# The first block's gate and up projections as two-level block products in quads, with the convolution by halves of tokens

## What is computed

```
D_FF = 2816
hn = rms_norm(h, norm_ffn_g)
gate = causal_depthwise_conv(hn @ w_ffn_gate, ffn_conv_w)      # 3 taps over tokens, per channel
h = h + (silu(gate) * (hn @ w_ffn_up)) @ w_ffn_down
```

## Time and profile before

| what | value |
|---|---|
| median of 3 runs | 3222.9 us (3221.6 to 3223.73) |
| span of the profiled execution, first to last instruction | 3218.1 us |
| median less that span | 4.8 us |
| PE, DVE, ACT, POOL busy over the span | 3120.3, 1809.7, 773.7, 1101.7 us |
| mean granted clock of PE | 0.989 of full speed |
| gate and up stage (L1936), first and last start | 806.1 and 1340.7 us |

### The profile page before, as it was taken

One profiled execution on the slowest core, in us unless ns is written; L12 is line 12 of the kernel. 1 busy time (PEld: TensorE's weight loads), 2 busy tenths in 40 slices (PEclk: granted clock), 3 DMA queues, 4 the chain that ended last, 5 costly groups with the idle time before them and its releaser, 6 DMA issues.

```text
span 3218.1 us, 32376 instructions
## 1 busy us (share of the span) xinstructions
PE 3120.3 (97%) x12306; PEld 1914.3 (59%) x12306; DVE 1809.7 (56%) x2558; ACT 773.7 (24%) x1302; POOL 1101.7 (34%) x855
## 2 busy tenths in 40 slices
PE   8997998999999999999999999999999999999997
PEld 3445564864444444588644554544554588888886
DVE  2386887742544434487634754753124655567877
ACT  3343334321111111000212333413212344410002
POOL 0010020003333333455610100152014698855655
PEclk9999999999999999999999999999999999999998
DMA  4220111241222122475312211102112233366652
GB/s 140 66 66 27 53 31 53 66 158 65 79 98 85 63 98 85 168 260 194 129 53 80 66 53 57 62 33 90 62 53 78 105 138 144 118 232 246 228 191 91
DMA packets 206121, 334.88 MB, mean 104 GB/s; under 512 B 10128, under 2 KB 123280, under 8 KB 205200
## 3 DMA queue, kind: packets, MB, share of 16 engines
q1 hardware_dynamic: 205968, 332.81, 29.8%
HBM read 268.55 MB, written 64.23 MB: 103 GB/s over the span
## 4 chain that ended last, share of the span: by engine, by line
PE 86%; DVE 8%; POOL 3%; ACT 2%; issue 1%; DMA 1%; DVEq 0%; POOLq 0%; SPq 0%; ACTq 0%
PE psum L1936 16%; PE psum L3767 15%; PE psum L181 10%; PE psum L3496 8%; PE psum L2555 8%; PE psum L407 7%; PE psum L1981 3%; PE psum L4334 3%; PE psum L563 1%; DVE arena L1380 1%; DVE arena L1378 1%; PE psum L3513 1%; PE psum L4311 1%; PE psum L4272 1%; PE psum L1987 1%
## 5 line engine op out<-in xcount | busy, mean ns | idle before, releaser
L3767 PE MATMUL psum<-arena 128*128 128x256 f32 x2660 | 579.4, 381 | 7.1 <-POOL arena L3793 7.1
L3767 PEld LDWEIGHTS psum<-arena 128*128 128x128 f32 x2660 | 506.7, 191 | 78.8 <-POOL arena L3793 8.6
L1936 PE MATMUL psum<-arena 128*128 128x512 f32 x1232 | 530.1, 592 | 1.9 <-DVE arena L2314 1.9
L1936 PEld LDWEIGHTS psum<-arena 128*128 128x128 f32 x1232 | 233.7, 190 | 296.6 <-issue 291.5
L407 PE MATMUL psum<-arena 128*128 128x512 f32 x768 | 337.9, 599 | 7.1 <-DVE arena L1236 4.9
L181 PE MATMUL psum<-arena 128*128 128x512 f32 x768 | 332.4, 592 | 1.5 <-ACT arena L4504 1.5
L2236 DVE TENSOR_TENSOR arena<-arena,psum 128x512 f32<-128x512 f32 x176 | 117.0, 686 | 296.3 <-PE psum L1936 154.7
L407 PEld LDWEIGHTS psum<-arena 128*128 128x128 f32 x768 | 146.2, 192 | 189.6 <-issue 185.0
L181 PEld LDWEIGHTS psum<-arena 128*128 128x128 f32 x768 | 145.8, 190 | 182.1 <-issue 180.6
L2555 PE MATMUL psum<-arena 128*128 128x512 f32 x576 | 251.7, 595 | 0.0
L3496 PE MATMUL psum<-arena 128*128 128x256 f32 x1080 | 244.6, 380 | 6.3 <-DVE arena L3541 5.6
(11 more groups left out here) (552 smaller groups left out, 4374.2 us busy)
## 6 DMA issues: line engine op xcount, KB each, us to landing
arena<-w_in SPq DMA_DIRECT2D x42, 1024.0 KB, 5.2
arena<-mlp_w SPq DMA_DIRECT2D x72, 512.0 KB, 7.0
arena<-w_ffn_down SPq DMA_DIRECT2D x36, 512.0 KB, 7.3
arena<-mlp_w SPq DMA_DIRECT2D x8, 2048.0 KB, 8.6
mlp_hidden_T<-arena SPq DMA_DIRECT2D x32, 512.0 KB, 2.6
arena<-mlp_hidden_T SPq DMA_DIRECT2D x16, 1024.0 KB, 5.6
arena<-w_out SPq DMA_DIRECT2D x12, 1024.0 KB, 5.2
mlp_hidden_B<-arena SPq DMA_DIRECT2D x24, 512.0 KB, 2.6
```

The costliest lines, as they stand in the source:

```text
L1936: mm = nc.tensor.matmul(ps, left, right, start=(k == 0), stop=(k == 3))
L3767: mm = self.env.nc.tensor.matmul(ps[:, 256 * r:256 * r + 256], left[:, s, r * P:(r + 1) * P], right[:, s, :], start=(first and s == 0 and ...
```

## The change

Gate and up become one product in the class `Quads`: a quad is 256 gate columns and the 256 up columns of the same pair, so eleven quads, quad 0 with plain items and ten with two levels. Items 1 and 2 of quad 1 run between those of quad 0. The loads are two of 1 MB per quad into one of two buffers. The seven items of a quad are added up on DVE (`combine`), seven sums of 128 x 1024.

The convolution is done per half of the tokens, for the two tiles of the pair: `conv(g, 0)` and `conv(g, 1)`. The second half needs the last two columns of the first, which are kept in `past`, and adds them with four small instructions. `silu` and `mul` are per half, too. The four sums of the hidden tile (T3, T1, T2, T4) move from POOL to DVE. The hidden tile and its sums have one buffer instead of three, so `conv(g, 0)` waits until pair g - 1 is stored. The order on DVE is written out by iteration n, where `added_after` says what follows an item: after an item of m1 = 1 both muls of the quad before, after 2 the four sums, after 6 U2 and C11, after 7 U3, after 5 U4 and C22, after 4 C21 and conv half 0, after 3 C12 and conv half 1. The first of these runs one iteration after its item, the others two.

The POOL queue now holds the level sums and outer sums of the quads. The rings reuse the table of constants, which is loaded again afterwards. The buffers of the down product move to other tiles, and what its loads and sums wait for changes: weights of items 0 and 1 are fetched when quad 9 is past. The first loads of "ple" wait for other events.

```
-            def conv(g, j):
-                i, from_, to = 2 * g + j, made["gate"][j], hid(j, g)
-                if g >= 3 and j == 0:
-                    dve.wait_ge(*stored(g - 3))
-                step.step(dve, v_.tensor_scalar(to, from_, tap(2, i), None, ALU.mult))
-                step.step(dve, v_.scalar_tensor_tensor(to[:, 1:T], from_[:, 0:T - 1], tap(1, i), to[:, 1:T], ALU.mult, ALU.add))
-                hidden.mark(v_.scalar_tensor_tensor(to[:, 2:T], from_[:, 0:T - 2], tap(0, i), to[:, 2:T], ALU.mult, ALU.add), "conv", g, j)
...
+            def conv(g, h):
+                if h == 0:
+                    if g:
+                        dve.wait_ge(*stored(g - 1))
...
+                hidden.wait(dve, ("C11", "C12")[h], g)
+                to, from_ = hid(h), (a_, c_)[h][g > 0]
+                taps = lambda j: [tap(j, 2 * g + r) for r in range(2)]
+                if h == 0:
+                    v_.tensor_copy(past, from_[:, :, HALF - 2:HALF])
+                for r in range(2):
+                    step.mark(v_.tensor_scalar(to[:, r, :], from_[:, r, :], taps(2)[r], None, ALU.mult))
+                base = step.n
+                for r in range(2):
+                    dve.wait_ge(tap_done, base - 1 + r)
+                    step.mark(v_.scalar_tensor_tensor(to[:, r, 1:], from_[:, r, 0:HALF - 1], taps(1)[r], to[:, r, 1:], ALU.mult, ALU.add))
+                for r in range(2):
+                    dve.wait_ge(tap_done, base + 1 + r)
+                    ins = v_.scalar_tensor_tensor(to[:, r, 2:], from_[:, r, 0:HALF - 2], taps(0)[r], to[:, r, 2:], ALU.mult, ALU.add)
+                if h:
+                    for r in range(2):
+                        step.mark(v_.scalar_tensor_tensor(to[:, r, 0:2], past[:, r, :], taps(0)[r], to[:, r, 0:2], ALU.mult, ALU.add))
+                    for r in range(2):
+                        dve.wait_ge(tap_done, base + 3 + r)
+                        ins = v_.scalar_tensor_tensor(to[:, r, 0:1], past[:, r, 1:2], taps(1)[r], to[:, r, 0:1], ALU.mult, ALU.add)
+                hidden.mark(ins, "conv", g, h)
...
+            added = [(name, q) for name in {6: ("U2", "C11"), 7: ("U3",), 5: ("U4", "C22"), 4: ("C21",), 3: ("C12",)}.get(m1, ())]
...
+            elif m1 in (3, 4):
+                added += {3: ends(q)[0:1] if q == 0 else ends(q)[1:2], 4: ends(q)[0:1] if q else []}[m1]
+            elif m1 in (1, 2):
+                added += {1: ends(q - 1)[2:4], 2: ends(q - 1)[4:]}[m1]
...
+            for n in range(LAST_N + 1):
+                if two_level(n - 1):
+                    quads.add_block(dve, n - 1, "c22")
...
+                for key in added_after(n - 2)[1:]:
+                    add_up(key)
+                if two_level(n):
+                    quads.add_block(dve, n, "c11")
+                    if n == LAST_N - 1:
+                        late.right_sums(dve, 0)
+                    quads.add_block(dve, n, "c12")
+                for key in added_after(n - 1)[:1]:
+                    add_up(key)
...
+            for q in PAIRS:
+                if q:
+                    store_pair(q - 1)
+                if q + 2 < 11:
+                    made_late.wait(sp, *quads.last_pass(at_item[q, 4]))
+                    p_sum.wait(sp, "S4", q)
+                    load_quad(q + 2)
+                elif q == 9:
+                    late.load_weights(sp, 0, before_late_load)
+                    late.load_weights(sp, 1, before_late_load)
```

More of the change, by code:

```diff
@@ L1832, in weights_of, with passed @@
             return down[:, q + 5 * c:q + 5 * c + n, j]
+        def passed(eng, m1):
+            made_late.wait(eng, *quads.last_pass(at_item[10, m1]))
         def before_late_bank(pe, at):
-            tiles.wait_free(pe, late_banks[at])
+            b = late_banks[at]
+            if at == 0:
+                tiles.wait_free(pe, b)
+                return
+            n, kind = max((n, m) for n in range(LAST_N - 3, LAST_N) for m in (1, 2, 3) if quads.bank_of(n, m) == b)
+            if kind == 1:
+                copy.wait(pe, "c21", n)
+            else:
+                hidden.wait(pe, {2: "c11", 3: "c12"}[kind], n)
@@ L2097, in _ @@
             hidden.wait(sp, "late", "S", 24)
-            load_unit(UNITS)
-            made_late.wait(sp, "late", 26, "all")
-            load_unit(UNITS + 1)
-            for v in range(UNITS + 2, len(sequence)):
-                after.wait(sp, *last_of(v - 2))
+            load_unit(0)
+            hidden.wait(sp, "late", "S", 25)
+            load_unit(1)
+            for v in range(2, len(ple_units)):
+                after.wait(sp, *ple_units[v - 2], 1)
                 load_unit(v)
@@ new lines, in combine @@
+            def combine(name, q):
+                a, b, c, d, e, f, b4 = [out_of(q, m1) for m1 in (1, 2, 6, 7, 5, 3, 4)]
+                before = {"C11": "U2", "U3": "C11", "U4": "U3", "C22": "U4", "C21": "C22", "C12": "C21"}
+                if name in before:
+                    hidden.wait(dve, before[name], q)
+                if name in ("U2", "U3", "U4", "C21", "C12"):
+                    quads.wait_product(dve, at_item[q, {"U2": 6, "U3": 7, "U4": 5, "C21": 4, "C12": 3}[name]])
+                to, one, two = {"U2": (c, a, c), "C11": (a, a, b), "U3": (d, c, d), "U4": (c, c, e), "C22": (e, d, e), "C21": (d, d, b4),
+                                "C12": (c, c, f)}[name]
+                hidden.mark(v_.tensor_tensor(to, one, two, ALU.add), name, q)
@@ L2420, in _, with more @@
-            for n in range(1, LATE):
+            def more(o):
+                made_late.wait(pool, *quads.last_pass(at_item[0, {"T3": 7, "T4": 4, "B22": 3}[o]]))
+                if o != "T4":
+                    hidden.wait(pool, "x", "T2", 1)
+                if o != "T3":
+                    hidden.wait(pool, "x", "T1", 1)
+                if o != "B22":
+                    pool.wait_ge(residual_out[0], residual_out[1] + 32)
+                quads.more_sums(g_, p_sum, pool, o)
+            add_sq(0, range(8))
```

575 lines of the change are left out of this document (306 added, 269 removed).

## The result

The changed kernel takes 3292.77 us (median of 4 runs, 3291.98 to 3293.28), the kernel before on the same chip 3222.25 (4 runs, 3220.01 to 3223.73): ratio 1.0219, 95% interval 1.0205 to 1.0234. The forecast was 3256 us and slower; the sign was right, the size was 37 us short, and the time lies 4.8 us above the range.

A forecast was written before the change was run, and what follows sets the result against it. PE was taken to bound the gate and up stage. 486.6 + 77 for DVE and its port + 5 for the tail = 568.6 against 535.0, +33.6, so 3256 us; range 3200 to 3288.

The forecast's parts named there:

- PE time removed: Gate and up stage: quad 0 at 48.1 us, ten quads at 42.6, norm about 2.1; PE work 476.1 us.
- bulge: PE's stall per quad from a late c22, as DVE and POOL take turns at SBUF; own range 6 to 10.5 us.
- the term "77 us": Gate and up stage: stalls of 8 us at nine places (quads 2 to 10) plus 5 for quad 0's convolution.
- start (quad 0's burst and quad 2's place): First quads of the stage: 5 us for quad 0's convolution among quad 1's items, 8 us for quad 2.
- the term 486.6: Gate and up stage without anything new: 476.1 us of PE work plus 10.5 of waiting, 48.4 less than before.
- my bound of 10.7: Stall at one place if nothing of POOL's passes under DVE's PSUM adds: 10.7 us; 0.5 if nothing is shared.
- the working: Stall at item (q, 2): DVE ends at 4.5 + 19.7 = 24.2 us, PE wants 15.5, so 8.7 us.
- The signs that I named: Stage over 535 us; 256-column matmuls near 0.217 apart except gaps of 3 and 5; taps 1.1 to 1.2; POOL stretched 15.
- The port costs little: Gate and up stage: PE held 1 us a quad or less; kernel at 3180 to 3190 us; chance 0.15.
- POOL becomes the pace: Gate and up stage: POOL's 44.8 us a quad sets the pace; stage 513.6, kernel 3202 us; chance 0.13.
- The tail goes worse: Down product: DRAM's round trip and the weights behind it cost 20 us more than forecast, 3276 us; chance 0.07.
- Loads, stores and ACT's copies at nothing: Gate and up stage: loads have 40 us to spare, copies are those of the second block; no cost.

The follow-up runs named there:

- e1: The changed kernel with the two earlier taps of the convolution left out, output not the reference's; 3182.18 us.
- e3: The changed kernel with dummy matmuls on PE ahead of its two long waits for c22, from the third quad on; 3285.25 us.
- spread kernel: The changed kernel with the convolution cut by rows over several DVE turns and C11 later, from the third quad on, same work; 3228.43 us.
- e5: The spread kernel with the last tap's scale on ACT for three of four rows a quad, all four in the first quad; 3222.83 us.
- e9: e5 with the first two quads spread by rows as well, the first convolution beginning one item earlier; 3216.49 us.
- e8: e5 with the sums T3 and C22 moved from DVE's fullest turns to emptier ones, from the fourth quad on; 3227.53 us.

## Why the prediction was right in sign and short in size

**PE time removed: right.** With its rivals for the port gone the stage is 493.7 us, against my 486.6 without bulge; the period is 42.56 against 42.6 a quad. PE was busy 481.5 us there, 5.4 above the 476.1 forecast, and waited 12.2 against 10.5. The 5.4 fit the clock, which the sum took as full: it is 0.74 from 886.9 to 900.0 and 0.87 from 916.4 to 930.0 in that kernel, behind waits of 5.5 and 2.7 us.

**The step that failed is the term "77 us" of the part on DVE and its port.** The stage holds 597.5 - 486.6 = 110.9 us in its place. By sections, against the kernel without taps:

| section | forecast | measured |
|---|---|---|
| base (stage of e1 less 486.6) | 0 | 7.1 |
| start (quad 0's burst and quad 2's place) | 5 + 8 | 15.8 |
| seven quads | 7 x 8 = 56 | 7 x 11.17 = 78.2 |
| last quad, to the down product | 8 | 9.8 |
| sum | 77 | 110.9 |

Without the base, which belongs to the term 486.6, the collision cost 103.8 us where 77 stood.

The mechanism is the one forecast: two engines by turns, c22 late at the items (q, 1) and (q, 2), PE released by L3656. The size per quad was 11.2, not 8, and even beyond my bound of 10.7. Of the 3.2 us missing per quad, 1.6 is the clock (period 53.7 against 52.1 with it kept up), a term that the sum did not have: I took every matmul at 0.2173. The other 1.6 is c22 itself: at full clock it costs 9.6 and not 8. 0.7 of that I gave away: the working came to 8.7 and I took 8 without a reason. The working itself was close. It has 19.7 us from S2 to the end of c22 of (q, 2), and at full clock it is 19.9 (e3); the pass behind it is 9.0 us late there. The last 0.6 come behind a c22 later in the quad, which I had not looked at. The waits as they stand in the profile (77.2 in the stage, 87.5 forecast with those of the start) look like a hit, but by chance: part of the bulge had become slow matmuls (520.75 us busy against 476.1), and these hid behind DVE.

**The signs that I named.** Gaps of "about 3 and 5": 3.04 and, in most quads, 3.3 to 3.9; right for the first. Taps at 1.1 to 1.2: 1.34. Adds from PSUM untouched: 0.417. POOL stretched by 15 us a quad: 266.5 us in seven quads are 38, 9 more than its 29.4. POOL waiting for PE: yes (2.69 before S2 above). The matmuls at 0.217 between gaps: wrong for 3.4 to 6.8 us behind most of the long gaps, where the clock is 0.50 (in the usual quad 3.4 behind the first and 6.8 behind the second).

**Rivals.** "The port costs little" fell with the result; its 3180 to 3190 is just where e1 came out, which is what the change would be worth without the collision. "POOL becomes the pace" fell with the waits: POOL is busy 266.5 of 382 us in the seven quads and waits for PE, and PE's waits there all name DVE's add; in e1, with all of POOL's sums, the period is 42.6. "The tail goes worse": the down product took 7.7 us more (forecast 5), not 20. 3.8 us more lie behind it: 2.4 in the second block's first MLP product (363.3 us against 360.9), 2.5 behind that, less 1.1 in between; their cause is open. Loads, stores and ACT's copies at nothing: right, but for 4.7 us in the start, where DVE waited for the first pair's store before it could write the next hidden half.

## What to carry to other kernels

When two engines take turns at a port, don't ask whether their busy times fit in the period; list what stands ahead of the instruction that the bound engine waits for, and spread that. Here the same instructions in other turns of the queue gave back 64 of 71 us. A wait behind which PE's clock falls costs more than its length, but not as much as the slow matmuls add up to when another engine is late meanwhile (here 1.6 us a quad came back, not 3): price it by keeping the clock up with dummies. Do not round a term of the sum down without a reason. And before moving an instruction to the emptiest turn of its engine, look at what the other user of the port has there.

## What the runs showed of the hardware

- A very small instruction of DVE with both tensors in SBUF can wait out a whole one of POOL. In the spread kernel an edge tap of one column took 2.27 us beside POOL's S3 of 2.36, against 0.22 alone. Timelines of DVE and POOL:

```profile
1074.89 2.27 DVE L2374 SCALAR_TENSOR_TENSOR arena<-small_sb,cols_sb,arena 128x1 f32<-128x1 f32 x1
```

```profile
1074.79 2.36 POOL L3723 TENSOR_TENSOR arena<-arena 128x1024 f32<-128x1024 f32 x1
```

- TENSOR_SCALAR with one tensor input takes its turns too: 1.03 us beside POOL, 0.479 without it.
- Whether the clock fell behind a wait did not go by the length of the wait alone. Two waits at the same place in two kernels, 2.13 us in e5 and 2.14 us in e9 (from the timelines), were followed by 0.62 in the first and by 1.00 in the second. Windows of e5, then of e9:

```profile
1319.60:1322.00 2.40, 2.40 (x7) 1.97 (x8) 2.16 (x2) 0.38 (x1) 2.40 (x2) 0.62 1.02 357
```

```profile
1313.80:1317.00 3.20, 3.20 (x15) 2.84 (x16) 2.48 (x3) 0.77 (x3) 3.12 (x3) 1.00 1.03 328
```

In e8, of eight waits of 1.84 to 1.90 us at the same place of a quad, those of 1.86 and 1.88 were followed by 0.50 and the others by 1.00. In the spread kernel's window above, with waits of up to 1.8 us, it stayed at 1.00; the wait of 3.07 us in the changed kernel was followed by 0.50.
